# Seven-product FFN blocks on one Trainium2 core: products and weight buffers by halves of the depth, and three left sums on GpSimd

## The chip, the cores and the metric

The kernel runs on one core of a Trainium2 chip. The metric is the device time of one execution in microseconds (us). The engines are TensorE (PE, matrix products), ScalarE (ACT), VectorE (DVE), GpSimd (POOL) and SyncE (SP, which issues DMAs).

## What is computed

The program is two transformer blocks one after the other, on 512 tokens of width 1024, all in float32. The first has a mixer and a mixture of experts, and the change leaves it alone. The second is a feed-forward network (FFN), a mixer and another FFN, each added to `x`. Only the two FFNs matter here:

```
def swiglu_ffn(x, w_gate, w_up, w_down):
    return (jax.nn.silu(x @ w_gate) * (x @ w_up)) @ w_down

x = x + 0.5 * swiglu_ffn(rmsnorm(x, ffn1_norm[l]), ffn1_w_gate[l], ffn1_w_up[l], ffn1_w_down[l])
x = x + hybrid_mixer(...)
x = x + 0.5 * swiglu_ffn(rmsnorm(x, ffn2_norm[l]), ffn2_w_gate[l], ffn2_w_up[l], ffn2_w_down[l])
```

`w_gate` and `w_up` are 1024 by 2816, `w_down` is 2816 by 1024.

## The kernel before, in words

**Three matmuls for one.** A float32 product is made of operands that are rounded into a high part and a rest: `hi` (ScalarE, `rounded`, L1939, a cast) and `lo` = raw - hi (VectorE, `rest`, L2386). Each product of 128 rows of depth is then three matmuls: high by high, high by low, low by high (L1600 to L1602).

**Sets of seven.** Most of an FFN is cut into sets, `SETS`: five gate-up sets `("gu", p, cut)` and two down sets `("s", p)`, in the order gu(0,1), s(0), gu(1,0), gu(1,1), s(1), gu(2,0), gu(2,1). A set is a 2 by 2 block product done as seven block products in the manner of Strassen and Winograd, so it needs sums of left blocks and sums of weight blocks. Product j (0 to 6) is `seven` (L1580): 512 of depth in four steps of 128, two row blocks t (tokens) of 128 rows, one PSUM bank each (`BANK[j] + t`), and 512 columns (384 in the last two sets). That is 24 matmuls: first all twelve of row block 0, then all twelve of row block 1. Products 3, 4, 5 and 6 add onto the banks of products 1, 3, 4 and 0 (`PAST`), and may start on a bank only when its content has been read: in a gate-up set by ScalarE's copies `R1`, `R2` (L2018), `R4`, in a down set by VectorE's additions into `x_sb` (`seven_x`, L2500). After product 6 of a down set its banks must be read the same way before product 0 of the next set.

**Weights.** A weight unit is 128 by 2048 (128 by 1536 in the last two sets). There are two pairs of `hi`/`lo` buffers, used in turn (`place_ffn`), so the unit of product j+1 may be cast only when product j-1 is done (`hl_free`). In the sets each unit is cast in two parts, both of which wait for that. Three units of a set are sums of weight blocks (T2, T1, T4; T3 too), made in place by DMAs that add, issued by GpSimd (`onto`, L1408).

**Left sums.** In a down set the left blocks are parts of the hidden matrix `HF8`. VectorE makes S3, and then in place S1, S2 and S4 (`sum_`, L2449 to L2457). Each of the seven lefts is then rounded by ScalarE (`sum_hi`, L2002) and VectorE (`sum_lo`, L2462) into one of three pairs of buffers, LB0 to LB2.

**The order** is a list of steps, written out by `schedule_ffn` (L665), from which each engine takes its own in that order, and an engine waits for its own step before it looks at the next. Around product j the list has: the casts and rests of unit j+1, product j, then `behind[j]`, the steps that read product j (copies, additions, `silu` as `sg` and `sgb`, gate times up as `ht` and `hb`) and the left sums. After product 0 of s(0), gu(1,1), s(1) and gu(2,1), TensorE turns two blocks of the hidden rows that `hb` (L2491, VectorE) makes, and after product 6 before such a set two that `ht` makes.

Of the kernel before, what the change touches and what calls it, by code (L numbers as in the profile page):

```python
# [110 lines left out]
class Unit:  # L111


    def __init__(self, key, src, kc, n):
        self.key, self.src, self.kc, self.n = key, src, kc, n
        self.raw = self.hi = self.lo = self.slot = self.done = self.made = self.four = None
        self.last = False
        self.raw_free, self.hl_free, self.lo_free = [], [], []


class Feed:

# [542 lines left out]
def schedule_ffn(S, feed, pre, order, name):  # L665
# [17 lines left out]
    feed.halves = True  # L683
    for what in SETS:
# [199 lines left out]
def program(nc, I, out):  # L884
# [15 lines left out]
    with ctx:  # L900
# [190 lines left out]
        a_sum, v_sum = sig("a_sum"), sig("v_sum")  # L1091
# [35 lines left out]
        def place_ffn(first, n, loads, at_raw, at_hl, at_fifth, own=()):  # L1127
# [25 lines left out]

        for group, first, n in ((p1, 0, len(p1)), (p2, first_moe, len(p2)), (p3, first3, len(p3)), (p5, first5, len(p5))):
# [202 lines left out]
        def pool_program(pool):  # L1357
# [79 lines left out]
            todo = {"m2_bias": m2_bias, "m2_row": m2_row, "seven": seven}  # L1437
# [103 lines left out]
        def pe_program(pe):  # L1541
# [38 lines left out]
            def seven(key, j, t, u):  # L1580
                q = U[u]
                b = BANK[j] + t
# [5 lines left out]
                if not more:  # L1588
                    taken(b)
                elif key[1] == "s":  # L1590
                    pe.wait_ge(v_sum, ("x", key[0], key[2], PAST[j], t))
                elif j == 6:
                    pe.wait_ge(v_ev, ("C22", *at_set(key), t))
                else:
                    pe.wait_ge(a_ev, ({3: "R1", 4: "R2", 5: "R4"}[j], *at_set(key), t))
                left_ready(pe, key, j)
                c = slice(t * 128, t * 128 + 128)
                o = PS[:, b, 0:q.n]
                for k in range(4):
                    e.matmul(o, xh[:, k, c], h[:, k, :], start=k == 0 and not more, stop=False, skip_group_check=more)  # L1600
                    e.matmul(o, xh[:, k, c], l[:, k, :], start=False, stop=False, skip_group_check=more)  # L1601
                    x = e.matmul(o, xl[:, k, c], h[:, k, :], start=False, stop=k == 3, skip_group_check=more)  # L1602
                x.then_inc(*p_mm((key, j, t)))
                if key[1] == "s":
                    freed[b] = [(v_sum, ("x", key[0], key[2], j, t))]
                elif j in (2, 5, 6):
                    freed[b] = [(v_ev, ({2: "C11", 5: "ht", 6: "C21"}[j], *at_set(key), t))]
# [318 lines left out]
        def act_program(act):  # L1926
            e = act.e

            def rounded(u, part=None):
# [7 lines left out]
                for s, k in q.hl_free:  # L1937
# [45 lines left out]
            def sum_hi(n, p, w):  # L1983
                if w[0] == "S":
                    act.wait_ge(v_sum, (w, n, p))
# [10 lines left out]
                else:  # L1996
# [378 lines left out]
        def dve_program(dve):  # L2375
# [64 lines left out]
            def sum_(n, p, w):  # L2440
# [750 lines left out]
```

## Time and profile before

| | |
|---|---|
| median of 3 runs | 1778.1 us (1777.47 to 1778.37) |
| the profiled execution | 1777.71 us, span 1775.9 us |
| mean granted TensorE clock | 0.995 |
| TensorE busy | 1721.1 us, 97% |
| VectorE busy | 1010.5 us, 57% |
| ScalarE busy | 704.5 us, 40% |
| GpSimd busy | 78.9 us, 4% |

The sets of the first FFN lie between 938 and 1206 us of the span, those of the second between 1466 and 1734 us. The shares are means over the whole span, over stages that differ.

### The profile page before, as it was taken

To read this page: it belongs to the slowest core of one execution; us is meant where nothing else is said; L and a number is where in the kernel's file an instruction comes from. 1 tells how busy PE (TensorE), PEld (TensorE's weight loads), DVE (VectorE), ACT (ScalarE), POOL (GpSimd) and SP (SyncE) were. 2 spreads that over 40 slices of the span, in tenths; PEclk is the share of its full clock that TensorE was granted. 3 is DMA by queue.
4 is the path that set the end of the run, shared out by engine and by line. 5 is a ranking of instruction groups with operands and counts; after the bars stand their busy time and mean duration, and the time that the engine had idled before them with its cause. 6 is when DMAs were issued, how large, how long until landed. Compare 5 with 4: busy or idle time off the path is not lost.

```text
span 1775.9 us, 21351 instructions
## 1 busy us (share of the span) xinstructions
PE 1721.1 (97%) x8703; PEld 1277.9 (72%) x8703; DVE 1010.5 (57%) x1489; ACT 704.5 (40%) x1144; POOL 78.9 (4%) x78
## 2 busy tenths in 40 slices
PE   7999999998999999999999999999999999999998
PEld 6878888885454545454477788898877887788896
DVE  4768865643333333333457866765577457856765
ACT  4556435441111111111335445454355435545453
POOL 0000000000000000000001111100000001111100
PEclk9999999998999999999999999999999999999999
DMA  6222225547999999999947888883303167898781
GB/s 216 94 72 72 95 81 180 193 154 289 421 421 420 421 421 421 420 421 421 372 122 170 213 201 196 179 190 124 119 0 107 49 194 185 192 220 196 166 200 56
DMA packets 117512, 385.74 MB, mean 217 GB/s; under 512 B 7088, under 2 KB 22592, under 8 KB 91424
## 3 DMA queue, kind: packets, MB, share of 16 engines
q1 hardware_dynamic: 88928, 318.33, 46.7%
q0 software_dynamic: 26176, 61.78, 18.9%
q10 hardware_dynamic: 2304, 4.20, 0.6%
q8 instruction: 71, 1.16, 0.3%
q14 instruction: 33, 0.27, 0.0%
HBM read 364.36 MB, written 6.29 MB: 209 GB/s over the span
## 4 chain that ended last, share of the span: by engine, by line
PE 85%; DVE 9%; ACT 5%; issue 1%; DMA 0%; SPq 0%; DVEq 0%; ACTq 0%
PE PS L1491 12%; PE PS L1600 8%; PE PS L1602 8%; PE PS L1601 8%; PE PS L1524 6%; PE PS L1630 6%; PE PS L1632 6%; PE PS L1631 6%; PE PS L1634 3%; PE PS L1636 3%; PE PS L1635 3%; DVE lo L2386 2%; PE PS L1462 2%; PE PS L1463 2%; PE PS L1534 2%; PE PS L1708 2%
## 5 line engine op out<-in xcount | busy, mean ns | idle before, releaser
L2386 DVE TENSOR_TENSOR lo<-raw,hi 128x1024 fp32r<-128x1024 f32 (+2 forms) x273 | 328.1, 1232 | 199.1 <-ACT hi L1939 195.6
L1939 ACT CAST hi<-raw 128x1024 fp32r<-128x1024 f32 (+2 forms) x275 | 282.4, 1066 | 220.9 <-PE PS L1602 142.9
L1600 PE MATMUL PS<-hi,xh_ffn 128*128 128x512 f32 (+1 forms) x320 | 118.5, 370 | 6.3 <-issue 4.0
L1602 PE MATMUL PS<-hi,xl_ffn 128*128 128x512 f32 (+1 forms) x320 | 117.6, 368 | 0.0
L1601 PE MATMUL PS<-lo,xh_ffn 128*128 128x512 f32 (+1 forms) x320 | 117.5, 367 | 0.0
L1491 PE MATMUL PS<-raw,XG 128*64 128x512 f32 x352 | 117.1, 593 | 0.0
L2346 DVE TENSOR_TENSOR HF<-SG,PS 128x512 f32<-128x512 f32 x16 | 17.4, 1090 | 164.8 <-PE PS L1491 164.8
L2361 DVE SCALAR_TENSOR_TENSOR YL<-PS,SM,YH 128x512 fp32r<-128x512 f32 x30 | 21.1, 746 | 138.8 <-ACT YH L1922 138.8
L2369 DVE TENSOR_TENSOR x_sb<-x_sb,PS 128x512 f32<-128x512 f32 x128 | 78.2, 678 | 8.7 <-PE PS L1535 8.7
L1905 ACT COPY HT<-PS 128x512 f32<-128x512 f32 x16 | 9.4, 586 | 175.1 <-PE PS L1500 175.1
L1634 PE MATMUL PS<-xTh,hi 128*128 128x512 f32 x192 | 78.3, 408 | 0.4 <-DVE lo L2386 0.3
L1491 PE MATMUL PS<-rawz,XG 128*64 128x512 f32 x280 | 77.7, 592 | 0.0
L1636 PE MATMUL PS<-xTh,lo 128*128 128x512 f32 x192 | 75.0, 391 | 0.0
L1635 PE MATMUL PS<-xTl,hi 128*128 128x512 f32 x192 | 75.0, 391 | 0.0
L1491 PEld LDWEIGHTS PS<-raw,XG 128*64 128x64 f32 x352 | 36.4, 137 | 49.6 <-issue 49.5
L1600 PEld LDWEIGHTS PS<-hi,xh_ffn 128*128 128x128 f32 x320 | 60.1, 188 | 15.6 <-issue 8.4
L1602 PEld LDWEIGHTS PS<-hi,xl_ffn 128*128 128x128 f32 x320 | 60.1, 188 | 7.6
L1462 PE MATMUL PS<-SE,hnh 128*128 128x256 f32 x256 | 65.2, 294 | 0.2 <-DVE SE L2319 0.2
L1601 PEld LDWEIGHTS PS<-lo,xh_ffn 128*128 128x128 f32 x320 | 60.1, 188 | 7.2
L1463 PE MATMUL PS<-SE,hnl 128*128 128x256 f32 x256 | 63.6, 287 | 0.0
L1922 ACT ACTIVATE YH<-PS,SM 128x512 fp32r<-128x512 f32 x30 | 19.0, 683 | 99.8 <-PE PS L1524 99.8
L1491 PEld LDWEIGHTS PS<-rawz,XG 128*64 128x64 f32 x280 | 24.8, 137 | 38.8 <-issue 38.8
(520 smaller groups left out, 4237.5 us busy)
## 6 DMA issues: line engine op xcount, KB each, us to landing
raw<-in_w_in SPq DMA_DIRECT2D x26, 1024.0 KB, 5.1
rawz<-in_w_down_experts SPq DMA_DIRECT2D x25, 1024.0 KB, 10.9
raw<-in_w_up_experts SPq DMA_DIRECT2D x24, 1024.0 KB, 16.0
raw<-in_w_gate_experts SPq DMA_DIRECT2D x20, 1024.0 KB, 15.5
raw<-in_ffn_w_down SPq DMA_DIRECT2D x20, 1024.0 KB, 6.0
rawz<-in_w_up_experts SPq DMA_DIRECT2D x19, 1024.0 KB, 19.1
raw<-in_w_down_experts SPq DMA_DIRECT2D x16, 1024.0 KB, 12.0
rawz<-in_w_gate_experts SPq DMA_DIRECT2D x16, 1024.0 KB, 13.8
```

Source lines behind the costliest of these rows:

```text
L1491: x = e.matmul(PS[64 * q:64 * q + 64, b, :], XG[(i // GP) % 2][:, k, s:s + 64], w[q][:, kk * 512:kk * 512 + 512], start=k == 0, stop=k == 7)
L1524: x = e.matmul(PS[64 * q:64 * q + 64, b + c, :], HT[:, j, 64 * q:64 * q + 64], w[q][:, jj * D + c * 512:jj * D + c * 512 + 512], start=j = ...
L1600: e.matmul(o, xh[:, k, c], h[:, k, :], start=k == 0 and not more, stop=False, skip_group_check=more)
L1601: e.matmul(o, xh[:, k, c], l[:, k, :], start=False, stop=False, skip_group_check=more)
L1602: x = e.matmul(o, xl[:, k, c], h[:, k, :], start=False, stop=k == 3, skip_group_check=more)
L1630: e.matmul(o, xh[:, k, c], h[:, kk, :], start=s0, stop=False)
L1631: e.matmul(o, xh[:, k, c], l[:, kk, :], start=False, stop=False)
L1634: e.matmul(o, h[:, kk, c], xh[:, k, :], start=s0, stop=False)
L1635: e.matmul(o, h[:, kk, c], xl[:, k, :], start=False, stop=False)
L1636: x = e.matmul(o, l[:, kk, c], xh[:, k, :], start=False, stop=s1)
L1939: e.copy(q.hi[:, a:b], q.raw[:, a:b]).then_inc(*a_hi((u, 0) if part == 0 else u))
L2386: e.tensor_tensor(q.lo[:, a:b], q.raw[:, a:b], q.hi[:, a:b].bitcast(F32), ALU.subtract).then_inc(*v_lo(key))
```

## The change

Products go by halves of the depth. TensorE now takes depth steps 0 and 1 for both row blocks and then steps 2 and 3 for both, waits for each half of the weights apart, and signals ("half") when it has done with the first half. The first part of the cast of a unit waits for that signal of the product two before. In the list, behind product j, now come the first parts of unit j+2 (`split_first`), then `behind[j]`, then the second parts of unit j+2. The units of the first set are cast in halves from the start. In the down sets GpSimd makes S1, S2 and S4; S2 is kept with the other sign, which the rounding turns back. S3, and the sums of the gate-up sets, stay on VectorE.

```
@@ class Feed @@
     def split_to(self, j):
         while self.split < min(j, len(self.units)):
-            if self.halves and self.units[self.split].four:
+            if self.units[self.split].four:
                 u = self.first + self.split
-                self.steps.extend([("hi", u, 0), ("hi", u, 1), ("lo", u, 0), ("lo", u, 1)])
+                if self.rounded:
+                    self.steps.extend([("hi", u, 1), ("lo", u, 1)])
+                else:
+                    self.steps.extend([("hi", u, 0), ("hi", u, 1), ("lo", u, 0), ("lo", u, 1)])
                 self.split += 1
+                self.rounded = False
                 continue
...
+    def split_first(self):
+        u = self.first + self.split
+        if self.split < len(self.units) and self.units[self.split].four:
+            self.steps.extend([("hi", u, 0), ("lo", u, 0)])
+            self.rounded = True
@@ schedule_ffn @@
         for j in range(7):
             u = feed.take((pre, *what))
             S.extend(ahead if j == 0 else ())
-            S.extend(("seven", (pre, *what), j, t, u) for t in range(2))
+            S.append(("seven", (pre, *what), j, u))
+            feed.split_first()
             S.extend(behind[j])
@@ place_ffn @@
                 u.hl_free = at_hl[j] if j < len(at_hl) else [U[first + j - 2].done]
+                if j >= len(at_hl) and U[first + j - 2].half and u.n <= U[first + j - 2].n:
+                    u.hl_first = [U[first + j - 2].half]
...
+        for f in fours.values():
+            for j, q in enumerate(f.plan):
+                q.half = (p_mm, (f.key, j, "half"))
@@ pool_program @@
+            def sum_(n, p, w):
+                if p == "x" or w == "S3":
+                    return
+                a11, a12, a21, a22 = (HF8[:, 4 * k:4 * k + 4, 256 * r:256 * r + 256] for r, k in ((0, 0), (0, 1), (1, 0), (1, 1)))
+                if w == "S1":
+                    pool.wait_ge(v_sum, ("S3", n, p))
+                    for tb in (2, 3):
+                        pool.wait_ge(a_ev, ("hT", n, p, 1, tb))
+                    e.tensor_tensor(a21, a22, a21, ALU.subtract).then_inc(*g_sum((w, n, p)))
+                elif w == "S2":
+                    pool.wait_ge(v_sum, ("A11l", n, p))
+                    pool.wait_ge(g_sum, ("S1", n, p))
+                    e.tensor_tensor(a11, a21, a11, ALU.add).then_inc(*g_sum((w, n, p)))
+                else:
+                    pool.wait_ge(v_sum, ("A12l", n, p))
+                    pool.wait_ge(g_sum, ("S2", n, p))
+                    e.tensor_tensor(a12, a11, a12, ALU.subtract).then_inc(*g_sum((w, n, p)))
@@ pe_program: seven @@
-                pe.wait_ge(a_hi, u)
-                pe.wait_ge(v_lo, u)
...
-                c = slice(t * 128, t * 128 + 128)
-                o = PS[:, b, 0:q.n]
-                for k in range(4):
...
+                for half in range(2):
+                    pe.wait_ge(a_hi, u if half else (u, 0))
+                    pe.wait_ge(v_lo, u if half else (u, 0))
+                    for t in range(2):
+                        b = BANK[j] + t
+                        if not half:
...
+                        c = slice(t * 128, t * 128 + 128)
+                        o = PS[:, b, 0:q.n]
+                        for k in (2 * half, 2 * half + 1):
...
+                        if half:
+                            x.then_inc(*p_mm((key, j, t)))
+                        elif t:
+                            x.then_inc(*p_mm((key, j, "half")))
@@ act_program: rounded @@
-                for s, k in q.hl_free:
+                for s, k in q.hl_first if part == 0 and q.hl_first else q.hl_free:
                     act.wait_ge(s, k)
@@ act_program: sum_hi @@
+                if w == "S2" and p != "x":
+                    e.activation(h, FROM[w], ACT.Copy, scale=-1.0).then_inc(*a_sum((w, n, p)))
+                    return
                 e.copy(h, FROM[w]).then_inc(*a_sum((w, n, p)))
@@ dve_program: sum_ @@
+                if p != "x" and w != "S3":
+                    return
@@ dve_program: sum_lo @@
+                if w == "S2" and p != "x":
+                    e.scalar_tensor_tensor(out=l, in0=FROM[w], scalar=-1.0, in1=h.bitcast(F32), op0=ALU.mult,
+                                           op1=ALU.subtract).then_inc(*v_sum((w + "l", n, p)))
+                    return
```

ScalarE, down set s(0) of the first FFN, around products 3 to 5: `hi` are casts of weight units (the wait names the queue or sum that brings the unit), `LB` casts of lefts. Before, and then with the change:

```order
L1939 CAST hi_53<-raw_51 128x1024 [waits p_product,d_w5]
L1939 CAST hi_53<-raw_51 128x1024
L2002 CAST LB2h<-HF_193 128x1024 [waits v_sum]
L1939 CAST hi_54<-raw_50 128x1024 [waits p_product,d_T4]
L1939 CAST hi_54<-raw_50 128x1024
L2002 CAST LB0h<-HF_193 128x1024 [waits a_evicted]
```

```order
L1979 CAST hi_53<-raw_51 128x1024 [waits p_product,d_w5]
L1979 CAST hi_53<-raw_51 128x1024 [waits p_product]
L1979 CAST hi_54<-raw_50 128x1024 [waits p_product,d_T4]
L2045 CAST LB2h<-HF_193 128x1024 [waits g_sum]
L1979 CAST hi_54<-raw_50 128x1024 [waits p_product]
L1979 CAST hi_53<-raw_180 128x1024 [waits p_product,d_T3]
L2045 CAST LB0h<-HF_193 128x1024 [waits a_evicted]
```

The first part of a unit (the one with a `d_` wait) has moved ahead of the `LB` cast and now has a product wait of its own, and the second part has another.

VectorE at the same place: `lo` are rests of units, `x_sb<-PS` are `seven_x`, `HF<-HF` is the sum S4. Before, and then with the change:

```order
L2386 TENSOR_TENSOR lo_56<-raw_49,hi_54 128x1024 [waits a_rounded] x2
L2457 SCALAR_TENSOR_TENSOR HF_193<-HF_193 128x4x256 [waits v_sum]
L2500 SCALAR_TENSOR_TENSOR x_sb<-PS,x_sb 128x512 [waits p_product] x2
L2386 TENSOR_TENSOR lo_55<-raw_51,hi_53 128x1024 [waits a_rounded] x2
L2462 TENSOR_TENSOR LB2l<-HF_193,LB2h 128x1024 [waits a_sum]
L2500 SCALAR_TENSOR_TENSOR x_sb<-PS,x_sb 128x512 [waits v_sum,p_product] x2
```

```order
L2429 TENSOR_TENSOR lo_56<-raw_49,hi_54 128x1024 [waits a_rounded]
L2429 TENSOR_TENSOR lo_55<-raw_51,hi_53 128x1024 [waits a_rounded]
L2549 SCALAR_TENSOR_TENSOR x_sb<-PS,x_sb 128x512 [waits p_product] x2
L2429 TENSOR_TENSOR lo_55<-raw_51,hi_53 128x1024 [waits a_rounded]
L2429 TENSOR_TENSOR lo_56<-raw_50,hi_54 128x1024 [waits a_rounded]
L2511 TENSOR_TENSOR LB2l<-HF_193,LB2h 128x1024 [waits a_sum]
L2549 SCALAR_TENSOR_TENSOR x_sb<-PS,x_sb 128x512 [waits v_sum,p_product] x2
```

S4 is gone, and a first-part rest stands ahead of each pair of `x_sb` additions, where before there were two rests of a unit whose wait ended a product earlier.

GpSimd in the same down set; `d_`-less rows with `v_rest` are T2, T1, T4. Before, and then with the change:

```order
L1408 DMA raw_52<-in_ffn_w_down 128x4x512 [waits v_rest]
L1408 DMA raw_49<-in_ffn_w_down 128x4x512 [waits v_rest]
L1408 DMA raw_50<-raw_52 128x2048 [waits d_T2,v_rest]
L1408 DMA raw_180<-in_ffn_w_up 128x4x512 [waits d_w13]
L1408 DMA raw_180<-in_ffn_w_gate 128x4x512 [waits v_rest]
```

```order
L1424 DMA raw_52<-in_ffn_w_down 128x4x512 [waits v_rest]
L1424 DMA raw_49<-in_ffn_w_down 128x4x512 [waits v_rest]
L1438 ISA
L1438 TENSOR_TENSOR HF_193<-HF_193 128x4x256 [waits a_evicted,v_sum]
L1442 TENSOR_TENSOR HF_193<-HF_193 128x4x256 [waits g_sum,v_sum]
L1424 DMA raw_50<-raw_52 128x2048 [waits d_T2,v_rest]
L1424 DMA raw_180<-in_ffn_w_up 128x4x512 [waits d_w13]
L1446 TENSOR_TENSOR HF_193<-HF_193 128x4x256 [waits g_sum,v_sum]
L1424 DMA raw_180<-in_ffn_w_gate 128x4x512 [waits v_rest]
```

S1 and S2 stand between T1 and T4, and S4 behind the T3 of the next set.

## Rows read from the trace of the kernel before

**Rows 1.** The page, part 1: busy time and share by engine.
```profile
PE 1721.1 (97%) x8703; PEld 1277.9 (72%) x8703; DVE 1010.5 (57%) x1489; ACT 704.5 (40%) x1144; POOL 78.9 (4%) x78
```

**Rows 2.** Windows over both FFNs' sets: window, length, busy of PE, PEld, DVE, ACT, POOL.
```profile
936.00:1210.00 274.00, 264.73 (x1279) 227.35 (x1278) 195.01 (x215) 142.91 (x188) 32.31 (x28) 1.00 0.84 194
1464.00:1740.00 276.00, 268.76 (x1299) 231.01 (x1298) 191.71 (x212) 142.74 (x187) 30.59 (x26) 1.00 0.82 189
```

**Rows 3.** TensorE's timeline, first matmuls of products: start, us, form [idle before <-releaser].
```profile
938.55 0.47 PE L1600 MATMUL PS<-hi,XS3h 128*128 128x512 f32 x1 [1.51 <-ACT hi L1939]
...
950.22 0.47 PE L1600 MATMUL PS<-hi,xh_ffn 128*128 128x512 f32 x1 [0.54 <-issue]
...
975.80 0.47 PE L1600 MATMUL PS<-hi,xh_ffn 128*128 128x512 f32 x1 [1.75 <-issue]
...
994.06 0.39 PE L1600 MATMUL PS<-hi,LB2h 128*128 128x512 f32 x1
...
1001.05 0.47 PE L1600 MATMUL PS<-hi,LB0h 128*128 128x512 f32 x1 [1.39 <-ACT hi L1939]
...
1007.44 0.47 PE L1600 MATMUL PS<-hi,LB1h 128*128 128x512 f32 x1 [0.68 <-DVE x_sb L2500]
...
1013.00 0.39 PE L1600 MATMUL PS<-hi,LB2h 128*128 128x512 f32 x1
...
1086.84 0.47 PE L1600 MATMUL PS<-hi,xh_ffn 128*128 128x512 f32 x1 [1.14 <-DVE lo L2386]
...
1503.54 0.47 PE L1600 MATMUL PS<-hi,xh_ffn 128*128 128x512 f32 x1 [1.75 <-issue]
```

**Rows 4.** TensorE's timeline: row blocks, a start behind turns, and a 384-column product.
```profile
978.64 0.39 PE L1600 MATMUL PS<-hi,xh_ffn 128*128 128x512 f32 x1
...
982.15 0.48 PE L1600 MATMUL PS<-hi,LB0h 128*128 128x512 f32 x1
...
1010.28 0.39 PE L1600 MATMUL PS<-hi,LB1h 128*128 128x512 f32 x1
...
1149.96 0.33 PE L1600 MATMUL PS<-hi,xh_ffn 128*128 128x384 f32 x1
...
1154.12 0.33 PE L1600 MATMUL PS<-hi,xh_ffn 128*128 128x384 f32 x1
```

**Rows 5.** ScalarE's timeline, start of down set s(0).
```profile
981.62 2.00 ACT L1939 CAST hi<-raw 128x1024 fp32r<-128x1024 f32 x2 [4.71 <-PE PS L1602]
983.52 1.06 ACT L1981 COPY HF<-PS 128x512 f32<-128x512 f32 x2
984.47 1.16 ACT L2037 ACTIVATE RB<-RB 128x512 f32<-128x512 f32 x2
```

**Rows 6.** VectorE's timeline, down set s(0).
```profile
981.56 0.69 DVE L2469 TENSOR_TENSOR RB<-RB,PS 128x512 f32<-128x512 f32 x1 [0.67 <-PE PS L1602]
982.70 2.36 DVE L2386 TENSOR_TENSOR lo<-raw,hi 128x1024 fp32r<-128x1024 f32 x2 [0.45 <-ACT hi L1939]
985.15 1.29 DVE L2491 SCALAR_TENSOR_TENSOR RB<-RA,RB 128x512 f32<-128x512 f32 x2
...
1005.47 1.22 DVE L2457 SCALAR_TENSOR_TENSOR HF<-HF 128x1024 f32<-128x1024 f32 x1
1006.61 1.28 DVE L2500 SCALAR_TENSOR_TENSOR x_sb<-PS,x_sb 128x512 f32<-128x512 f32 x2
...
1010.21 1.22 DVE L2462 TENSOR_TENSOR LB2l<-HF,LB2h 128x1024 fp32r<-128x1024 f32 x1
```

**Rows 7.** GpSimd's timeline: its one large sum before the change.
```profile
1261.26 2.40 POOL L1397 TENSOR_TENSOR Bt<-Bt,C 128x1024 f32<-128x1024 f32 x1 [4.77 <-DMA Bt<-in_rel_tile]
```

**Rows 8.** ScalarE's timeline in gate-up sets gu(1,0), gu(1,1) and gu(2,0).
```profile
1043.41 0.56 ACT L2018 COPY RB<-PS 128x512 f32<-128x512 f32 x1
...
1082.16 1.05 ACT L2002 CAST LB0h<-S3f 128x1024 fp32r<-128x1024 f32 x1 [4.82 <-DVE S3f L2449]
...
1158.53 1.57 ACT L1939 CAST hi<-raw 128x768 fp32r<-128x768 f32 x2 [2.27 <-PE PS L1602]
```

More of the change, by code:

```diff
@@ L115, in __init__ @@
         self.key, self.src, self.kc, self.n = key, src, kc, n
-        self.raw = self.hi = self.lo = self.slot = self.done = self.made = self.four = None
+        self.raw = self.hi = self.lo = self.slot = self.done = self.half = self.made = self.four = None
         self.last = False
         self.raw_free, self.hl_free, self.lo_free = [], [], []
+        self.hl_first = None
 class Feed:
@@ L126, in __init__ @@
         self.split = self.taken = 0
-        self.spread, self.rounded, self.halves = False, False, False
+        self.spread, self.rounded = False, False
     def split_hi(self):
@@ L682, in schedule_ffn @@
     past = None
-    feed.halves = True
     for what in SETS:
@@ L1435, in seven @@
                     row("n2")
-            todo = {"m2_bias": m2_bias, "m2_row": m2_row, "seven": seven}
+            todo = {"m2_bias": m2_bias, "m2_row": m2_row, "seven": seven, "sum": sum_}
             for name, *a in after:
@@ L1578, in turn_hidden, with seven @@
                 freed[b] = [(v_ev, ("h", n, p, cut, tb))] if p == NS else [(a_ev, ("hT", n, p, cut, tb))]
-            def seven(key, j, t, u):
+            def seven(key, j, u):
                 q = U[u]
-                b = BANK[j] + t
                 h, l = (x[:, 0:4 * q.n].rearrange("p (k n) -> p k n", k=4) for x in (q.hi, q.lo))
                 xh, xl = (LEFT_H if key[1] == "s" else LEFT_X)[j]
-                pe.wait_ge(a_hi, u)
-                pe.wait_ge(v_lo, u)
                 more = j in PAST
[L1588 to L1595, printed above, removed]
-                left_ready(pe, key, j)
-                c = slice(t * 128, t * 128 + 128)
-                o = PS[:, b, 0:q.n]
-                for k in range(4):
[L1600 to L1607, printed above, removed]
@@ new lines, in seven @@
+                left_ready(pe, key, j)
+                for half in range(2):
[4 more added lines that the diff above has]
+                        if not half:
+                            if not more:
+                                taken(b)
+                            elif key[1] == "s":
+                                pe.wait_ge(v_sum, ("x", key[0], key[2], PAST[j], t))
+                            elif j == 6:
+                                pe.wait_ge(v_ev, ("C22", *at_set(key), t))
+                            else:
+                                pe.wait_ge(a_ev, ({3: "R1", 4: "R2", 5: "R4"}[j], *at_set(key), t))
+                        c = slice(t * 128, t * 128 + 128)
+                        o = PS[:, b, 0:q.n]
+                        for k in (2 * half, 2 * half + 1):
+                            e.matmul(o, xh[:, k, c], h[:, k, :], start=k == 0 and not more, stop=False, skip_group_check=more)
+                            e.matmul(o, xh[:, k, c], l[:, k, :], start=False, stop=False, skip_group_check=more)
+                            x = e.matmul(o, xl[:, k, c], h[:, k, :], start=False, stop=k == 3, skip_group_check=more)
+                        if half:
+                            x.then_inc(*p_mm((key, j, t)))
+                        elif t:
+                            x.then_inc(*p_mm((key, j, "half")))
@@ L1609, in mm @@
+                for t in range(2):
+                    b = BANK[j] + t
+                    if key[1] == "s":
+                        freed[b] = [(v_sum, ("x", key[0], key[2], j, t))]
+                    elif j in (2, 5, 6):
+                        freed[b] = [(v_ev, ({2: "C11", 5: "ht", 6: "C21"}[j], *at_set(key), t))]
             def mm(key, ui, i, u, a=0, b=None):
@@ L2445, in sum_ @@
                 else:
-                    for tb in range(NB) if w == "S3" else (2, 3):
-                        dve.wait_ge(a_ev, ("hT", n, p, 0 if w == "S3" else 1, tb))
+                    for tb in range(NB):
+                        dve.wait_ge(a_ev, ("hT", n, p, 0, tb))
                 if w == "S3":
```

8 lines of the change are left out of this document (3 added, 5 removed).

## The prediction

> **What bounds the kernel now.** The page's shares come first: TensorE is busy for 97% of the span [rows 1]. More work for it is not in the change, so a gain can only come out of its idle time. The windows over the sets give that: 274.00 - 264.73 = 9.3 us idle in the first FFN, 276.00 - 268.76 = 7.2 us in the second [rows 2]. The reader should see there too that VectorE is busy for 70% of these stretches and ScalarE for 52%: neither is full, but both work through one list, so what matters is what stands ahead of what.
>
> Then TensorE's timeline, first matmuls of products [rows 3]. A product that waits for nothing takes 5.44 us, and its row blocks 2.72 each (1010.28 to 1013.00) [rows 3, 4]. Over three products of the down set s(0) the starts are 994.06, 1001.05, 1007.44, 1013.00: 18.94 us where 16.32 would do, so 2.6 us lost. Unit 3's rests come too late (1.39 idle), then `seven_x` (0.68), and the first matmul after a wait costs some 0.08 more (0.47 in place of 0.39). The same pattern stands in all four down sets. In the first set of an FFN product 6 waits, 1.9 us by starts; in the first FFN also products 0 and 2 (1.7 and 0.7 by starts). In gu(1,1) product 4 waits, 1.3 [rows 3]. By starts the whole loss is 4.5 (first set, first FFN) + 2.0 (second) + 4 x 2.6 + 2 x 1.4 = 19.7 us. No change of these waits can give more.
>
> **The change: what goes.** Half a unit instead of a whole one gates a product, and the first half may be cast 2.72 us earlier. In the first set this takes away every wait listed: product 0 needs the first half only, and the unit of product 6 is no longer behind S3, A11 and a whole unit's cast. -4.5 and -2.0 us. In the down sets the wait of product 3 for its unit goes as well: VectorE is rid of three sums of 1.22 us [rows 6].
>
> **What comes: copies and additions that are late.** The price is in two places.
>
> First, row block 0 now ends at 4.08 us of its product (three quarters) and not at 2.72, and block 1's matmuls of the next product begin at 1.36 and not at 2.72. Between a bank's last matmul and its next use by the following product there are 1.36 us where there were 2.72.
>
> Second, every engine takes its steps in order, and ahead of the reading of product j there is now the first part of unit j+2, which cannot start before the half signal. Time from the start of a product: the half ends at 2.72; ScalarE starts 0.25 behind the end of a product (978.64 + 2.72 = 981.36, cast at 981.62) [rows 4, 5], so the cast runs from 2.97 to 4.02; VectorE's rest follows at 4.05 (0.03 behind, 981.62 + 1.05 to 982.70), and its next operation at 5.19 (two rests take 2.36, so 1.14 each back to back) [rows 5, 6]. Only then can the additions read a bank. From this:
> - **Down set, product 4**: addition 5.19 to 5.87 (0.68, half of the pair of 1.28 and its tail), TensorE 0.15 later (1006.61 + 0.68 to 1007.44) [rows 3, 6]: start at 6.02 in place of 5.44, and 0.08: 0.66 lost.
> - **Product 5**: S4's rounding stands between. Its rest adds 1.14: 7.16, 1.80 lost.
> - **Product 6** waits for the rest of A22: 5.19 + 1.22 + 0.15 = 6.56, 1.20 lost.
> - **Product 0 of the next set** waits for product 6's additions: 0.66 again. Before gu(2,0) the units are narrower (two parts cast in 1.57, not 2.00 [rows 5, 8]), and this and product 6 lose about 0.9 less together.
> - **Product 1 of s(0), s(1), gu(1,1) and gu(2,1)**: `sgb` and `hb` wait behind the cast and the rest. The first `hb` ends at 5.87, the second at 6.47; TensorE turns them at 5.98 and 6.58, 0.4 each (half the 0.79 from 981.36 to 982.15 [rows 4]), so it is free at 6.98 and not at 6.23: 0.74.
> - **Gate-up sets, product 4**: `sg` twice at 0.53 [rows 5] and `R2`, 0.58 (half the pair of 1.06 and its tail) [rows 5, 8], follow the cast's slot that ends at 3.92: 5.56, and 0.12: 0.24 + 0.08 = 0.3 lost, in gu(1,0), gu(2,0), gu(2,1). The narrow sets take 4.16 for a product [rows 4], but their casts shrink alike. In gu(0,1) turns lie between and hide it.
> - **gu(1,1), product 4**: S3 (1.22), its cast (the idle 4.82 before it [rows 8]) and three casts now stand before `sg`: `R2` ends 6.69 after product 3's start, so 1.45 lost, where 1.4 was lost before.
> - **Product 0 of s(0)**: VectorE is behind by S3, A11 and their rests from gu(0,1). Followed in the same way from product 4 on, product 6's first addition `C21` ends 1.6 after the product, behind turns that take 0.8: 1.05 lost.
>
> **GpSimd's sums.** One of the same size takes 2.40 [rows 7]. S1 cannot start before the turned rows of product 0 are copied, about 7.8 after the set's start; S2 is ready at 12.65, its rounding at 15.0, and product 3 starts at 17.9: nothing on the path. T4 goes out 2 us later than now and is needed 12 us after. No row shows GpSimd and VectorE at work on SBUF together. If neither disturbs the other, the cost is 0. If a VectorE operation with two SBUF inputs must wait for a whole GpSimd sum, and the reverse, then following the queue S2 ends at 13.9, S4 runs 16.2 to 18.6, and VectorE reaches product 3's addition at 25.5 and not 23.1: product 4 starts 2.3 us later still, in each of four sets. Between 0 and 2.3 I take 1.2, the nearest row: what S4 costs VectorE now (1.22 [rows 6]), since there is no idle time left behind it.
>
> The Trainium skill (SBUF — State Buffer, "SBUF: two separate sides") speaks for the upper end: VectorE with two SBUF inputs and a GpSimd operation that reads SBUF share a pair of ports under an exclusive lock, and the loser waits for the whole instruction. By that rule the result would be rival B's. No run here shows it yet.
>
> **The sum**, in us against the profiled execution (1777.7):
> - first sets: -4.5 + 1.05 and -2.0 + 1.05: -4.4
> - s(0) twice: 0.74 + 0.66 + 1.80 + 1.20 + 0.66 = 5.1, less 2.6: +5.0
> - s(1) twice: 4.2 less 2.6: +3.2
> - gu(1,0): +0.6; gu(1,1): 0.74 + 1.45 less 1.4: +1.6; gu(2,0) and gu(2,1): +0.4 and +1.1, twice: +3.0
> - GpSimd beside VectorE: 4 x 1.2: +4.8
>
> Together +13.8: 1791.5. That execution stands 0.4 us below the median of the runs shown, so 1791.9. Cast and rest instructions that are now split in the first set, and the waits at each half, cost nothing: TensorE goes from bank to bank without idle time now (1010.28) [rows 4].
>
> **The rivals.**
> - **A. The two engines don't disturb each other.** For it: nothing in the trace against. The sum without the last line is 1787.1. Chance 0.27.
> - **B. Full waiting.** The upper end, 4 x 2.3: 1777.7 + 9.0 + 9.2 + 0.4 = 1796.3. For it: S1 and S2 fall where VectorE has two rests to do, and behind S4 no idle time is left in the walk above. This is the rule of the Trainium skill's page named above. Chance 0.28.
> - **C. Faster: the additions keep up.** The place is the 1.36 us between a bank's end and its next use, less 0.20 and 0.15 to hand it over and back: 1.01, and an addition takes 0.68. It decides if VectorE is free at 4.6 of the product. That needs the rest of unit j+2 to be through 0.6 us sooner, or the half signal to leave before its last matmul ends. Then all of 19.7 goes: 1758; with half of the new waits left, 1768. Against it: 2.97 + 1.05 is already 4.02 before the rest begins. Chance 0.07.
> - **D. The new waits come out half as large**, because casts and additions overlap better than my walk in single steps says; gain and loss cancel: 1778. Chance 0.08.
> - **E. The halves do nothing**, since the wait for "half" is met late anyway. Then only VectorE's three sums are gone, which gives back at most the 1.6 us before product 3 of each down set (1001.05 - 994.06 - 5.44) [rows 3]: 1772 to 1778. The order shows a product wait at each half cast, so this has 0.02.
>
> **How the numbers follow.** The forecast, with contention in between, has 0.28 and is 1792. A and B lie close on both sides, and their chances spread by a few us each. The range from 1780 to 1801 holds all three and the upper part of D; below it lie C, E and half of D, above it a backlog larger than B's, together under 0.2. A difference of 0.2%, 3.6 us, is about what a measurement of this kernel can tell from none. Faster by more: C, E and a little of D, 0.09. Within: the rest of D and the low edge of A, 0.08. Slower: 0.83.
>
> **What would show it.** In TensorE's timeline: no wait at products 0, 2 and 6 of gu(0,1); none at product 3 of down sets; new ones at products 4, 5, 6 of down sets and 0 of the next, near 0.6, 1.7, 1.1 and 0.6 us, released by VectorE; in gate-up sets small ones at product 4 released by ScalarE's `RB`. TensorE's idle time in the two windows near 28 us together and not 16.5. `HF` on GpSimd: 12 sums near 2.4 us; rests on VectorE beside them at 1.2 (A), or with idle time or a duration up to 2.4 more (B). If the starts of products 4 and 5 of a down set lie 5.44 apart, the walk through the queues is wrong.

## The result

| | before | after |
|---|---|---|
| median | 1777.8 us (1776.7 to 1778.4, 4 runs) | 1804.7 us (1803.7 to 1805.5, 4 runs) |
| profiled span | 1775.9 us | 1803.0 us |
| granted clock | 0.995 | 0.992 |

The ratio is 1.0152, 95% interval 1.0134 to 1.017: slower by 27 us. The forecast was 1792, the upper end of its range 1801. The direction was right and the loss almost twice as large.

The shares, first lines of the page of after, beside [rows 1]:

```profile
PE 1732.0 (96%) x8703; PEld 1279.1 (71%) x8703; DVE 1026.5 (57%) x1479; ACT 713.8 (40%) x1146; POOL 110.5 (6%) x90
```

The same 8703 matmuls are busy for 10.9 us more, and VectorE, which gave away 12 sums of 1.22 us, is busy for 16 us more. Both say that single instructions became longer. The windows over the sets of after, beside [rows 2] (columns as there):

```profile
936.00:1222.00 286.00, 269.99 (x1273) 227.92 (x1272) 200.38 (x208) 146.75 (x187) 47.90 (x34) 0.99 0.80 186
1478.00:1766.00 288.00, 272.03 (x1283) 229.59 (x1282) 199.04 (x205) 147.46 (x187) 46.57 (x32) 0.99 0.78 179
```

Idle time of TensorE is 16.0 and 16.0 us, 32 together, where 16.5 was before and 28 foretold. Each window is 12 us longer than the one of before, and of that 5.3 and 3.3 us are busy time.

TensorE's timeline in s(0) of after, against [rows 3] and [rows 4]: the first matmul of product 0, the turns before product 1, products 3, 4, 5, 6, product 0 of the next set; last, product 4 of gu(1,1) and products 3 to 6 of s(1).

```profile
976.92 0.47 PE L1635 MATMUL PS<-hi,LB0h 128*128 128x512 f32 x1 [0.68 <-DVE RB L2518]
...
982.95 1.26 PE L1608 MATMUL PS<-C,RB 128*128 128x128 f32 x8 [0.34 <-DVE RB L2540]
...
997.18 0.47 PE L1635 MATMUL PS<-hi,LB0h 128*128 128x512 f32 x1 [2.06 <-DVE x_sb L2549]
...
1005.25 0.47 PE L1635 MATMUL PS<-hi,LB1h 128*128 128x512 f32 x1 [2.36 <-DVE x_sb L2549]
...
1014.11 0.47 PE L1635 MATMUL PS<-hi,LB2h 128*128 128x512 f32 x1 [1.55 <-DVE x_sb L2549]
...
1020.71 0.49 PE L1635 MATMUL PS<-hi,LB0h 128*128 128x512 f32 x1 [0.87 <-DVE LB0l L2511]
...
1026.85 0.47 PE L1635 MATMUL PS<-hi,XS3h 128*128 128x512 f32 x1 [0.43 <-DVE x_sb L2549]
...
1091.02 0.47 PE L1635 MATMUL PS<-hi,xh_ffn 128*128 128x512 f32 x1 [1.21 <-DVE lo L2429]
...
1128.49 0.47 PE L1635 MATMUL PS<-hi,LB0h 128*128 128x512 f32 x1 [2.02 <-DVE x_sb L2549]
...
1136.56 0.47 PE L1635 MATMUL PS<-hi,LB1h 128*128 128x512 f32 x1 [0.76 <-DVE x_sb L2549]
...
1143.81 0.47 PE L1635 MATMUL PS<-hi,LB2h 128*128 128x512 f32 x1 [1.56 <-DVE x_sb L2549]
...
1149.99 0.50 PE L1635 MATMUL PS<-hi,LB0h 128*128 128x512 f32 x1 [0.48 <-DVE LB0l L2511]
```

The waits of products 0, 2 and 6 of the first set are gone, and product 3 no longer waits for its unit. What came is a row of waits for VectorE, for its additions above all (product 6 for the rest of A22). Start to start, less 5.44 (for product 1 less the turns' 0.79 too; before the change this was 0.1 for product 1, 1.6 for 3, 1.0 for 4 and 0.1 or nothing for the others). The foretold values count the 0.08 us of a first matmul behind a wait at its own product; in the starts it shows one product later:

| product of a down set | foretold | after s(0) | after s(1) | h5 s(0), no sums |
|---|---|---|---|---|
| 1 (turns) | 0.74 | 0.8 | 0.8 | 0.8 |
| 3 | 0 | 2.2 | 2.2 | 0 |
| 4 | 0.66 | 2.63 | 2.63 | 0.59 |
| 5 | 1.80 | 3.42 | 1.81 | 1.82 |
| 6 | 1.20 | 1.16 | 0.74 | 1.12 |
| 0 of the next set | 0.66 | 0.70 | 0.28 | 0.74 |

(1014.11 - 1005.25 - 5.44 = 3.42, and so on.) Three cells stand out in s(0), products 3, 4 and 5. They are the places of GpSimd's sums and of what follows on them. Here is GpSimd in s(0) of after: S1, S2, the issues of T4 and T3, S4 (columns: start, duration, engine, line and tiles, count, idle time before it and its releaser).

```profile
985.00 2.40 POOL L1438 TENSOR_TENSOR HF<-HF 128x1024 f32<-128x1024 f32 x1 [4.93 <-ACT HF L2021]
987.55 3.19 POOL L1442 TENSOR_TENSOR HF<-HF 128x1024 f32<-128x1024 f32 x1
990.68 0.88 POOL L1424 DMA_DIRECT2D raw<-raw  x1
991.29 1.62 POOL L1424 DMA_DIRECT2D raw<-in_ffn_w_up  x1
992.08 3.26 POOL L1446 TENSOR_TENSOR HF<-HF 128x1024 f32<-128x1024 f32 x1
```

and VectorE beside it, against [rows 6]: the rests of two halves, S2's rest, and the additions of product 1, whose banks product 3 takes over.

```profile
985.81 6.01 DVE L2429 TENSOR_TENSOR lo<-raw,hi 128x1024 fp32r<-128x1024 f32 x2 [1.19 <-ACT hi L1979]
991.87 4.56 DVE L2508 SCALAR_TENSOR_TENSOR LB0l<-HF,LB0h 128x1024 fp32r<-128x1024 f32 x1
996.35 1.28 DVE L2549 SCALAR_TENSOR_TENSOR x_sb<-PS,x_sb 128x512 f32<-128x512 f32 x2
```

Two rests take 6.01 us in place of 2.36, and S2's rest 4.56 in place of 1.22: 3.65 + 3.34 = 7.0 us late by the addition of 996.35, and product 3 starts 0.8 after that began (997.18). The wait for the other engine stands inside the duration of the instruction that waits, not in its idle time. The times fit whole instructions: S1 ends at 987.40, the second rest (3.42 us long) begins at 988.4, S2 ends at 990.74, and both rests are done at 991.82, 1.1 later.

The Trainium skill (SBUF — State Buffer, "SBUF: two separate sides") says that VectorE with two SBUF inputs and GpSimd share a port pair under an exclusive lock, and that the loser waits for the whole instruction. The trace agrees as to whole instructions (6.01 for 2.36). It says too that the one that starts first has the lock. S2's rest starts at 991.87 by its record, 0.21 us ahead of S4's record, and still ends 1.1 after S4. Which of the two asked first can't be read from the records. S4's record itself begins while GpSimd still issues T3 (991.29 + 1.62 = 992.91); from there to S4's end are 2.4 us, its usual length. So S4's length fits that issue and not a wait for VectorE (in h6, below, S4 begins behind the issue and takes 2.40), and the rest had stood for 1.0 us by then. The issue alone doesn't hold a rest up: in h6 S2's rest at 993.02 lies beside it up to 994.06 and takes 1.23. Why the rest waited for S4 here stays open.

ScalarE's casts beside the sums keep their 1.05, though S2's cast has to wait for the sum:

```profile
987.05 1.05 ACT L1979 CAST hi<-raw 128x1024 fp32r<-128x1024 f32 x1 [1.27 <-PE PS L1637]
990.77 1.06 ACT L2043 ACTIVATE LB0h<-HF 128x1024 fp32r<-128x1024 f32 x1 [2.67 <-POOL HF L1442]
```

Last, the clock, in windows of after behind the wait of product 4 (columns as [rows 2]: PEclk is the third from the end):

```profile
1006.60:1009.70 3.10, 3.10 (x9) 2.37 (x8) 0.23 (x1) 0.00 (x0) 0.00 (x0) 0.51 1.04 367
1009.90:1012.00 2.10, 2.10 (x11) 1.74 (x10) 1.00 (x1) 2.00 (x2) 0.00 (x0) 1.00 0.76 291
```

TensorE runs at 1.2 GHz (0.51) and then at 2.4 GHz again. The first wait of s(0) (2.06) left the clock alone; behind the second (2.36) it fell 1 us into product 4. In s(0) this is the 1.6 us by which product 5 is later than in h5 (8.86 against 7.26 from product 4's start). In s(1) it fell one product earlier, behind the wait of 2.02, and costs nothing: product 4 waits for VectorE anyway, only 0.76 us now and not 2.36, and both sets have 8.07 between the starts of products 3 and 4.

Over the two FFNs, the growth read off fixed matmuls (product 0 of gu(0,1) to the first matmul of the last piece, `th_ffn`) is 13.2 and 15.5 us, 28.7 together. In the first FFN before the change this is counted from 936.88, where product 0 would have begun without its wait of 1.7. In after it begins at 935.30: the stages ahead took 1.6 us less in this execution, which leaves 27.1, the difference of the two spans.

### The profile page after: what moved, and what is told of

Its sections match the earlier page's. It is cut to its first block, busy times and chain, and to the rows that moved or that the text cites. A ratio compares the mean times of both kernels' runs of the same rounds, so it can differ in the third digit from the quotient of the medians.

```text
span 1803.0 us, 21515 instructions
## 1 busy us (share of the span) xinstructions
PE 1732.0 (96%) x8703; PEld 1279.1 (71%) x8703; DVE 1026.5 (57%) x1479; ACT 713.8 (40%) x1146; POOL 110.5 (6%) x90
## 4 chain that ended last, share of the span: by engine, by line
PE 80%; DVE 10%; ACT 6%; issue 2%; POOL 1%; DMA 0%; SPq 0%; DVEq 0%; ACTq 0%; POOLq 0%
PE PS L1523 12%; PE PS L1635 7%; PE PS L1637 6%; PE PS L1636 6%; PE PS L1556 6%; PE PS L1670 6%; PE PS L1672 5%; PE PS L1671 5%; PE PS L1674 3%; PE PS L1676 3%; PE PS L1675 3%; DVE lo L2429 3%; ACT hi L1979 2%; PE PS L1494 2%; PE PS L1566 2%
## 5 line engine op out<-in xcount | busy, mean ns | idle before, releaser
L2429 DVE TENSOR_TENSOR lo<-raw,hi 128x1024 fp32r<-128x1024 f32 (+2 forms) x275 | 349.1, 1279 | 256.6 <-ACT hi L1979 252.3
L1979 ACT CAST hi<-raw 128x1024 fp32r<-128x1024 f32 (+2 forms) x277 | 290.8, 1058 | 294.8 <-PE PS L1637 217.8
L1566 PE MATMUL PS<-YH,ST 128*128 128x512 f32 x128 | 52.2, 408 | 0.5 <-DVE YL L2395 0.5
```

Of the source, the lines that this page charges most:

```text
L1979: e.copy(q.hi[:, a:b], q.raw[:, a:b]).then_inc(*a_hi((u, 0) if part == 0 else u))
L2429: e.tensor_tensor(q.lo[:, a:b], q.raw[:, a:b], q.hi[:, a:b].bitcast(F32), ALU.subtract).then_inc(*v_lo(key))
```

## The experiments

Times are medians, ratios to the kernel before with 95% intervals.

**h1: GpSimd's part undone**, the halves kept. S1, S2 and S4 on VectorE as before.

```
-        a_sum, v_sum, g_sum = sig("a_sum"), sig("v_sum"), sig("g_sum")
+        a_sum, v_sum = sig("a_sum"), sig("v_sum")
@@ dve_program: sum_ @@
-                if p != "x" and w != "S3":
-                    return
```

> The change without its GpSimd part: halves as changed, S1, S2 and S4 made by VectorE as before. My theory has two causes: banks that are read late because the first-part cast stands ahead of the readers (about 9 us over the kernel before, 1787), and GpSimd and VectorE that shut each other out of SBUF, with TensorE's clock halved behind the long waits (the other 18 us). The sums on VectorE bring back 3.7 us of its work per down set, just where it is late, so I expect 1790 to 1800, with no VectorE rest above 1.3 us. Rival, GpSimd is the whole cause: 1778 or less.

Measured 1805.1 (1804.1 to 1808.5), ratio 1.0161 (1.0144 to 1.0178). The expectation missed: the sums on VectorE cost as much as on GpSimd. Product 3 doesn't wait now, and product 4 waits longer than anywhere else:

```profile
994.88 0.39 PE L1635 MATMUL PS<-hi,LB0h 128*128 128x512 f32 x1
...
1003.97 0.77 PE L1635 MATMUL PS<-hi,LB1h 128*128 128x512 f32 x1 [3.46 <-DVE x_sb L2540]
1004.54 0.63 PE L1636 MATMUL PS<-lo,LB1h 128*128 128x512 f32 x1
```

VectorE up to there, in the same kernel:

```profile
998.54 1.28 DVE L2540 SCALAR_TENSOR_TENSOR x_sb<-PS,x_sb 128x512 f32<-128x512 f32 x2
999.74 2.35 DVE L2426 TENSOR_TENSOR lo<-raw,hi 128x1024 fp32r<-128x1024 f32 x2
1002.00 1.22 DVE L2497 SCALAR_TENSOR_TENSOR HF<-HF 128x1024 f32<-128x1024 f32 x1
1003.14 1.28 DVE L2540 SCALAR_TENSOR_TENSOR x_sb<-PS,x_sb 128x512 f32<-128x512 f32 x2
```

It has no idle time; the two rests and S4 (3.4 us) stand in front of the additions that free a bank. So the change's two parts aren't a loss of 9 and one of 18 us: with the halves in this order, VectorE's list is too long either way.

**h2: GpSimd's part alone**, on the kernel before (whole products).

```
@@ pool_program, on the kernel before @@
+            def sum_(n, p, w):
...
+                    e.tensor_tensor(a21, a22, a21, ALU.subtract).then_inc(*g_sum((w, n, p)))
@@ dve_program: sum_ @@
+                if p != "x" and w != "S3":
+                    return
```

> The kernel before with its order and whole products, and only S1, S2 and S4 moved to GpSimd. If the two engines shut each other out, a rest of VectorE beside a GpSimd sum lasts 3 us or more, S2's rest comes late, and product 3 of each down set starts 1 to 3 us later than now: 1781 to 1790. If GpSimd only relieves VectorE, the waits before products 3 and 4 shrink by up to 2 us a set: 1770 to 1775.

Measured 1784.9 (1783.6 to 1787.0), ratio 1.0043 (1.0029 to 1.0057), as expected. The pair of rests is as long here (VectorE), and product 2 waits for it (TensorE), in a kernel without halves:

```profile
988.84 5.99 DVE L2407 TENSOR_TENSOR lo<-raw,hi 128x1024 fp32r<-128x1024 f32 x2 [2.55 <-ACT hi L1957]
994.87 1.23 DVE L2486 SCALAR_TENSOR_TENSOR LB0l<-HF,LB0h 128x1024 fp32r<-128x1024 f32 x1
```

```profile
994.93 0.47 PE L1618 MATMUL PS<-hi,LB2h 128*128 128x512 f32 x1 [2.26 <-issue]
...
996.57 0.63 PE L1618 MATMUL PS<-hi,LB2h 128*128 128x512 f32 x1
```

No wait of TensorE follows from S4 here, and the wait of product 4 [rows 3] is gone in exchange. The second row shows the halved clock again, behind a wait of 2.26 us. Product 3 follows product 2 by 7.17 us in all four down sets: in three of them product 2 runs partly at the halved clock, and in the s(0) of the second FFN, where the clock held, product 3 waits 1.49 us for its unit. So that wait is not gone, the slower clock covers it. A down set is 1.9 us longer than before.

**h3 and h4: the first parts late.** One line moved: the first part of unit j+2 goes behind the steps that read product j. h3 with GpSimd's sums, h4 with VectorE's.

```
             S.append(("seven", (pre, *what), j, u))
-            feed.split_first()
             S.extend(behind[j])
+            feed.split_first()
```

> The changed kernel with one line moved: the first parts of unit j+2 stand behind the steps that read product j, not ahead of them. If the place in the order is what costs, the waits before products 5 and 6 of down sets (1.7, 1.0), before product 0 behind them (0.6), before product 1 (0.5) and the 0.2 to 0.4 in gate-up sets go, some 15 to 20 us of the 27: 1783 to 1790, and what is left is GpSimd's. Rival, the halved distance between a bank's end and its next use (1.36 us) costs by itself: then these waits stay within 0.3 us of what they are, above 1797.

> Both causes taken away: first parts behind the readers, and S1, S2 and S4 on VectorE. Theory: the waits of the first set stay away (-6.5), those of product 3 in down sets shrink since half a unit is enough, and no rest is over 1.3 us: 1763 to 1773, below the kernel before. Rival, halved distance costs by itself: above 1778.

h3: 1782.5 (1779.2 to 1783.8), ratio 1.0026 (1.0016 to 1.0035), just below its expectation. h4: 1773.7 (1771.2 to 1776.1), ratio 0.9979 (0.9969 to 0.9988), just above it. One line is worth 22 us beside GpSimd's sums and 31 us without (h1 to h4). In h3 the waits of products 1, 5, 6 and 0 of the next set are gone with the order, so they came from it and not from the shorter way from a bank's end to its next use. Its one large wait is GpSimd's:

```profile
1000.24 0.58 PE L1635 MATMUL PS<-hi,LB0h 128*128 128x512 f32 x1 [3.02 <-DVE lo L2429]
```

```profile
987.95 6.02 DVE L2429 TENSOR_TENSOR lo<-raw,hi 128x1024 fp32r<-128x1024 f32 x2 [3.16 <-ACT hi L1979]
...
996.35 4.76 DVE L2429 TENSOR_TENSOR lo<-raw,hi 128x1024 fp32r<-128x1024 f32 x2
```

Between h3 and h4 lie 8.9 us: with this order GpSimd's sums cost 2.2 us a down set.

In h4 the down sets are as long as in the kernel before (41.74 and 41.73 us from product 0 of s(0) to product 0 of the next set). The half unit takes 1.0 us off product 3 (0.58 late by starts, 1.55 before), and product 4 is later by the same (1.92, 0.95 before), since S4 still stands ahead of the additions it waits for. The 4 us that h4 gains come from the first sets.

```profile
1003.96 0.47 PE L1635 MATMUL PS<-hi,LB1h 128*128 128x512 f32 x1 [1.64 <-DVE x_sb L2540]
```

**h5: no S1, S2, S4 at all.** Leaves out these sums in the down sets; the lefts are rounded from blocks that were not summed. All else as in after.

```
@@ pool_program @@
-            def sum_(n, p, w):
...
-            todo = {"m2_bias": m2_bias, "m2_row": m2_row, "seven": seven, "sum": sum_}
+            todo = {"m2_bias": m2_bias, "m2_row": m2_row, "seven": seven}
```

> The changed kernel with S1, S2 and S4 of the down sets not made at all, by neither engine (the lefts are rounded from the unsummed blocks, so that part of the computation is left out). It shows what the new order and the halves cost by themselves: my walk through the queues without anything between GpSimd and VectorE gave 1787 (rival A of the prediction). No wait over 2 us, so no halved clock. If it stays above 1797, the order costs more than I worked out and GpSimd less.

Measured 1786.2 (1785.2 to 1786.5), ratio 1.0044 (1.0029 to 1.006). Rival A, the sum without GpSimd's line, was 1787.1, and the table above has its waits place by place. TensorE in s(0), products 4, 5, 6 and the next 0:

```profile
1002.36 0.47 PE L1617 MATMUL PS<-hi,LB1h 128*128 128x512 f32 x1 [0.43 <-DVE x_sb L2536]
...
1009.62 0.47 PE L1617 MATMUL PS<-hi,LB2h 128*128 128x512 f32 x1 [1.56 <-DVE x_sb L2536]
...
1016.18 0.50 PE L1617 MATMUL PS<-hi,LB0h 128*128 128x512 f32 x1 [0.87 <-DVE LB0l L2498]
...
1022.36 0.47 PE L1617 MATMUL PS<-hi,XS3h 128*128 128x512 f32 x1 [0.43 <-DVE x_sb L2536]
```

So in after GpSimd's sums cost 1804.7 - 1786.2 = 18.5 us, 4.6 a down set.

**h6: S4 held back** until S2's rest is through.

```
-                    pool.wait_ge(v_sum, ("A12l", n, p))
+                    pool.wait_ge(v_sum, ("S2l", n, p))
```

> The changed kernel with one wait replaced: GpSimd's S4 starts only when VectorE's rest of S2 is done. If the two shut each other out by whole instructions, that rest falls from 4.6 to 1.2 us and the wait of 2.2 us before product 3 goes, and S4 now stands against the rests of units 3 and 4, so part of it comes back at product 4: 1795 to 1802. If the rest was long for another reason (its operation, its place in memory), it stays above 3 us and the time at 1804.

Measured 1798.9 (1797.6 to 1799.6), ratio 1.0119 (1.0103 to 1.0134), as expected. The rest of S2 is 1.23 us again, S4 2.40, and the wait of product 3 is gone; the rests behind pay for S4 (3.59 for two), and product 4 waits 2.58:

```profile
993.02 1.23 DVE L2508 SCALAR_TENSOR_TENSOR LB0l<-HF,LB0h 128x1024 fp32r<-128x1024 f32 x1
994.16 1.28 DVE L2549 SCALAR_TENSOR_TENSOR x_sb<-PS,x_sb 128x512 f32<-128x512 f32 x2
995.36 3.59 DVE L2429 TENSOR_TENSOR lo<-raw,hi 128x1024 fp32r<-128x1024 f32 x2
```

The additions, with one input in PSUM, started 0.17 us before S4 (994.33) and keep their 1.28, though the second of the pair runs beside it. The clock, which fell in all four sets of after, falls in s(1) alone, behind the wait of product 4. S4 falling on S2's rest thus cost 5.8 us, 1.5 a set on average; that holds what the clock did, and by starts s(0) is 3.7 us shorter than in after and s(1) 0.5 to 0.7.

**h8: the idle time filled.** Nine matmuls whose result nobody reads, ahead of products 3 and 4 of the down sets, to keep TensorE at work during its waits.

```
+                if key[1] == "s" and j in (3, 4):
+                    taken(6)
+                    for _ in range(9):
+                        e.matmul(PS[:, 6, :], fxh[:, 0, 0:128], fxh[:, 0, :], start=True, stop=True)
```

> The changed kernel with nine products of no use, on a free bank, ahead of the waits of products 3 and 4 in each down set, so that TensorE is not idle there. If the clock falls to half behind the long waits because TensorE was idle, it stays near 2.4 GHz now, the waits stay as long in sum, and some 1.6 us a set come back: 1797 to 1800. If the clock falls for another reason, or costs nothing: 1804 or more.

Measured 1803.6 (1803.3 to 1804.0), ratio 1.0145 (1.0129 to 1.016): 1.1 us less than after, where 5 to 8 were expected. The clock of the execution is 0.995. In s(0) the filling does what was said, 7.27 us from product 4 to 5 and not 8.86:

```profile
1006.81 0.47 PE L1639 MATMUL PS<-hi,LB1h 128*128 128x512 f32 x1 [0.31 <-DVE x_sb L2553]
...
1014.08 0.47 PE L1639 MATMUL PS<-hi,LB2h 128*128 128x512 f32 x1 [1.56 <-DVE x_sb L2553]
```

In s(1) nothing came back, since there the wait for VectorE takes what the clock gives. That leaves 3.1 us in two sets. The stages ahead of gu(0,1) were 1.5 us longer in this execution than in after's, as they vary between kernels that don't differ there (the first matmul of gu(0,1) lies at 935.35 in h7 and at 936.67 in h5). That gives the 1.6 us between the two spans (1803.0 and 1801.4). So the sets gave back 3.1 us, and the medians, 1.1 apart, don't show all of it.

**h7: the order mended.** The halves, all sums on VectorE, first parts late but for the three places where a unit is otherwise late; product 3's additions ahead of S4, product 0's behind it; S3 and A11 one product earlier in gu(1,1).

```
-                j = 2 if p else 4
+                j = 1 if p else 4
...
-            behind[3].append(("sum", pre, p, "S4"))
...
-            for j, js in ((1, (1,)), (2, (0,)), (3, (3,)), (4, (4,)), (5, (5, 2)), (6, (6,))):
+            for j, js in ((1, (1,)), (3, (3,)), (4, (4,)), (5, (5, 2)), (6, (6,))):
                 behind[j].extend(("seven_x", pre, p, q, t) for q in js for t in range(2))
+            behind[3].append(("sum", pre, p, "S4"))
+            behind[3].extend(("seven_x", pre, p, 0, t) for t in range(2))
...
-            feed.split_first()
+            early = (what == ("gu", 0, 1) and j in (0, 4)) or (what[0] == "s" and j == 1)
+            if early:
+                feed.split_first()
             S.extend(behind[j])
+            if not early:
+                feed.split_first()
```

> A version meant to beat both: halves, sums on VectorE, first parts behind the readers except at products 0 and 4 of the first set and product 1 of down sets, product 3's additions ahead of S4, product 0's behind it, and S3 and A11 one product earlier in gu(1,1). From the version with first parts behind the readers (1773.7) it should take the waits before products 3 and 4 of down sets (0.6 + 1.8, of which 0.3 stays), product 4 of gu(1,1) (1.2) and products 2 and 6 of the first set (0.5 + 0.8): 1758 to 1765. If the halved distance between a bank's end and its next use costs by itself, some of these waits stay: above 1769.

Measured **1765.4** (1764.3 to 1768.0), ratio **0.9932** (0.9918 to 0.9945), 12 us faster than before and a little above what was expected. One wait is left in the sets, at product 5 of each down set:

```profile
1006.21 0.47 PE L1640 MATMUL PS<-hi,LB2h 128*128 128x512 f32 x1 [1.49 <-DVE x_sb L2545]
```

**h9: the same order, whole products.** The kernel before with the lines of h7's edit that have no halves in them.

> The kernel before, whole products and all sums on VectorE, with only the changes of order that h7 has besides the halves: x3's additions ahead of S4, S3 and A11 of the second gate-up set one product earlier. Theory: of h7's 12.4 us the order brings 5 to 7 (about 0.8 at product 4 of four down sets and 1.3 at product 4 of two gu(1,1)), and the halves bring the rest, since only they take away the waits of the first sets (6.5 us). That gives 1770 to 1774, with the waits of the first set's products 0, 2 and 6 and product 3's in the down sets still there. Rival: the order alone does it all and the halves bring nothing: 1764 to 1767.

Measured 1779.4 (1777.8 to 1781.6), ratio 1.0009 (1.0 to 1.0018). Both theories missed. The order brings nothing to whole products. The wait of product 4 of gu(1,1) is gone (-1.3, twice), and the one at product 4 of the down sets has only moved to product 5 and grown, by 1.1 us four times, behind the unit's wait at product 3, which stays:

```profile
1000.97 0.47 PE L1601 MATMUL PS<-hi,LB0h 128*128 128x512 f32 x1 [1.43 <-ACT hi L1940]
...
1013.90 0.47 PE L1601 MATMUL PS<-hi,LB2h 128*128 128x512 f32 x1 [1.77 <-DVE x_sb L2501]
```

At that order the halves are worth 14.0 us (to h7): some 6.5 in the first sets and 1.7 in each of the four down sets, nearly all of it at product 3.

**h10: the mended order with GpSimd's sums**, S4 behind S2's rest.

> h7 with S1, S2 and S4 of the down sets on GpSimd again (S4 behind S2's rests). Theory: the two engines wait for each other, so what VectorE gets back (three sums of 1.22 us a set) it loses in its rests beside GpSimd's sums, and what is late falls on TensorE: 1767 to 1775, a loss of 0.5 to 2.5 us in each of four down sets. Rival: with the order mended VectorE's relief comes through and takes away the wait of product 5 (1.65 us in each of the four): 1758 to 1763.

Measured 1766.2 (1765.9 to 1767.5), ratio 0.9934 (0.9921 to 0.9948): the same as h7, 0.8 us above it, which their spreads don't tell apart. That lies just below what was expected, and the rival, that VectorE's relief takes away the wait of product 5, didn't come either. The engines wait for each other as much as ever (VectorE, three rests in 7.14 us):

```profile
985.74 7.14 DVE L2434 TENSOR_TENSOR lo<-raw,hi 128x1024 fp32r<-128x1024 f32 x3 [3.42 <-ACT hi L1984]
992.81 1.21 DVE L2513 SCALAR_TENSOR_TENSOR LB0l<-HF,LB0h 128x1024 fp32r<-128x1024 f32 x1
993.94 1.27 DVE L2554 SCALAR_TENSOR_TENSOR x_sb<-PS,x_sb 128x512 f32<-128x512 f32 x2
```

but nothing needed soon stands behind them, and TensorE's waits, inside product 3 (for the rest of its second half), at product 4 and at product 5, lengthen a down set to 41.25 us where h7's takes 41.15.

## Why the prediction was right in sign and wrong in size

By its own steps, in us over both FFNs; what was found is read from the starts of the sets' first matmuls:

| step | foretold | found |
|---|---|---|
| first sets, product 0 of s(0) with them | -4.4 | -5.0 |
| s(0) twice, order and halves | +5.0 | h5: +4.7 |
| s(1) twice, the same | +3.2 | h5: +2.9 |
| gu(1,0), gu(1,1), gu(2,x) | +5.2 | +5.8 |
| GpSimd beside VectorE | +4.8 (0 to 9.2) | +20.2 against h5 (+18.5 by the medians) |

- **The walk through the queues was right.** h5 has nothing but it, and gives 1786.2 against 1787.1; its waits at products 4, 5, 6 and 0 are 0.59, 1.82, 1.12, 0.74 against 0.66, 1.80, 1.20, 0.66. Product 0 of s(0) was a little overstated (1.05, found 0.92). The three waits of the first set as listed (1.9, 1.7, 0.7) add up to 4.3 and not 4.5; by starts 4.6 went in the first FFN, first matmuls included.
- **Cause of the new waits**: two were named, less time between a bank's end and its next use, and a first part that stands ahead of the reading. h3 and h7 show that the second decides: with the reading first they vanish, at the same spacing.
- **The step that failed is "GpSimd's sums".** That they wait for each other had been weighed as rival B, and is so. The value was taken between 0 and 2.3 a set, and it is 4.6. Three things were not in the bound. S4 was placed at 16.2 of the set, behind S2's rest; it came with it and made it 4.56 us long (1.5 a set by h6, clock included). A delay of VectorE was taken to be paid once, at product 4; it is paid at product 3 as well, since the 7.0 us reach the additions of product 1, and again at product 4. And the clock, halved behind such waits: 1.6 us in each s(0). By the table, against h5, that is 2.2 + 2.0 + 1.6 = 5.8 in s(0) and 2.2 + 2.0 = 4.2 in s(1), 20 us in all. The medians differ by 18.5; the stages ahead of the sets took 1.4 us less in after's execution than in h5's (first matmul of gu(0,1) at 935.30 and 936.67), which makes up the difference.
- **"VectorE is rid of three sums" was given as a reason why product 3's wait for its unit goes.** It isn't the reason: in h1 VectorE keeps the sums, and product 3 doesn't wait there either (0.00). The half unit takes the wait away, and the sums on VectorE cost their time at product 4 (3.65). What GpSimd's waiting costs is of the same size (1805.1 and 1804.7).
- **Rival C** (faster, the additions keep up) was given 1758 and 0.07. As the change stands it is wrong; with another order (h7, 1765.4) 12 of its 20 us are there.
- **Rival E**, that the halves do nothing, is wrong: 14.0 us between h9 and h7.

## What to carry to other kernels

When work is cut finer so that it can start earlier, put the new early steps behind those that free a buffer the bottleneck engine waits for: with the sums on VectorE the same halves cost 27 us (h1) or brought 4 (h4), by where one line stood, and with the order around them mended as well they brought 14 (h7 against h9). A sum moved from VectorE to GpSimd need not be free while VectorE has instructions with two SBUF inputs to do: it cost 4.6 us a down set in after, 2.2 in h3 and nothing that could be told in h10, by what stood behind the delayed instructions. Bound it by whole instructions of the other engine at each meeting, follow the delay to every product that waits for that engine, and look for it in durations, not in idle time. Behind a wait of TensorE of 2 us or more, reckon in this kernel with 1.5 us more for the halved clock (behind 3.2 us and more it fell in 8 of 8 places, below that in some), unless another wait follows close behind and swallows it.

## What the hardware showed that was not expected

- GpSimd's sum of 2.40 us lasts 3.19 where it meets VectorE's rests (S2); S4's 3.26 fits the DMA issue that its record overlaps by 0.83 us. A rest of 1.22 lasts up to 4.56. Additions with an input in PSUM (1.28 a pair) and ScalarE's casts (1.05) keep their time.
- TensorE's clock falls to 1.2 GHz (0.51) behind a single wait in a stage that is 94% busy, and stays there for 3 to 5 us. By the four down sets of each kernel, with waits counted by starts: behind waits of 3.2 to 3.6 us it fell every time (h1, h3); behind 2.4 to 2.8 in three of four (h2) and in two of four (h6); in after behind the 2.2 of product 3 in both s(1), and in both s(0) only behind the 2.5 of product 4 that followed; behind 1.9 and less (h4, h5, h7, h9) never. Outside the down sets it fell once, in h9, behind the 2.0 us before product 0 of gu(0,1). It costs 1.5 us where no wait follows. Filling the waits keeps it at 2.4 GHz (h8, clock 0.995). What decides below 3.2 us is open.
